# Router entry of a two-layer hybrid block: raw rows of x transposed, logits in four column groups from modulated weights, root and shift applied to the logits

## The reference, cut to what matters

```python
x_lat = x_lat + g1[:, None] * mix_x
hx2 = modulate(rmsnorm(x_lat, norm2_g[l]), sh2[:, None], sc2[:, None])   # h * (1 + scale) + shift
x_lat = x_lat + g2[:, None] * ec_moe(hx2, router_w[l], moe_w1[l], moe_w3[l], moe_w2[l])
...
aff = softmax(h @ router_w)                    # T x 16, fp32
gate, idx = top_k(swapaxes(aff, 1, 2), cap)    # cap = 32 tokens for each of 16 experts
```

## Time and profile before

| | |
|---|---|
| median of 3 runs | 2163.38 us (2161.03 to 2164.16) |
| profiled execution, span | 2163.4 us |
| TensorE busy | 1878.2 us, 87% |
| VectorE, ScalarE, GpSimd busy | 709.9, 444.8, 109.4 us |
| read from HBM | 560.27 MB, 259 GB/s over the span |

### The profile page before, as it was taken

One profiled execution on the slowest core, in us unless ns is written; L12 is line 12 of the kernel. 1 busy time (PEld: TensorE's weight loads), 2 busy tenths in 40 slices (PEclk: granted clock), 3 DMA queues, 4 the chain that ended last, 5 costly groups with the idle time before them and its releaser, 6 DMA issues.

```text
span 2163.4 us, 24879 instructions
## 1 busy us (share of the span) xinstructions
PE 1878.2 (87%) x9978; PEld 1123.9 (52%) x9978; DVE 709.9 (33%) x1130; ACT 444.8 (21%) x792; POOL 109.4 (5%) x150
## 2 busy tenths in 40 slices
PE   5999999999999799999999899999997666666654
PEld 3888756666777533333333488877886221112111
DVE  2273354433334512221222454455445100001001
ACT  2322333332222310000000332343333000000000
POOL 2070000000000000000000231000000000000000
PEclk9999999999999899999999999999999777778687
DMA  9423334234446489999999853444687899999996
GB/s 307 118 78 98 93 103 126 80 114 128 133 146 244 177 332 422 422 422 422 422 422 422 268 163 88 123 135 118 196 235 282 351 422 421 421 421 422 422 422 263
DMA packets 268871, 562.66 MB, mean 260 GB/s; under 512 B 11964, under 2 KB 208620, under 8 KB 219628
## 3 DMA queue, kind: packets, MB, share of 16 engines
q1 hardware_dynamic: 266412, 554.14, 68.2%
q0 software_dynamic: 1824, 5.12, 1.3%
q10 hardware_dynamic: 544, 2.10, 0.2%
HBM read 560.27 MB, written 1.05 MB: 259 GB/s over the span
## 4 chain that ended last, share of the span: by engine, by line
PE 68%; DMA 22%; DVE 5%; issue 2%; SPq 1%; ACT 1%; POOL 1%; POOLq 0%; DVEq 0%; ACTq 0%
PE PS L677 44%; PE PS L1096 17%; DMA nab<-in_moe_w 13%; DMA e_wr<-in_moe_w 6%; PE PS L738 2%; DMA ring<-in_w_mod 2%; PE PS L1047 2%; PE PS L871 1%; SPq L655 1%; DVE wr L1514 1%; PE PS L759 1%; PE PS L1074 0%; DVE arena L1560 0%; DVE arena L1819 0%; PE PS L1057 0%
## 5 line engine op out<-in xcount | busy, mean ns | idle before, releaser
L677 PE MATMUL PS<-hTr,wr 128*128 128x512 f32 (+1 forms) x2688 | 515.0, 348 | 5.2 <-DVE hTr L1548 5.2
L677 PEld LDWEIGHTS PS<-hTr,wr 128*128 128x128 f32 x2688 | 428.1, 190 | 72.5 <-issue 10.7
L1096 PE MATMUL PS<-arena 128*32 128x512 f32 (+1 forms) x960 | 305.1, 704 | 81.8 <-DMA nab<-in_moe_w 39.0
L1514 DVE TENSOR_TENSOR wr<-ring,wr 128x1024 fp32r<-128x1024 f32 x152 | 187.8, 1237 | 226.4 <-ACT wr L1162 226.2
L1162 ACT ACTIVATE wr<-ring 128x1024 fp32r<-128x1024 f32 x152 | 160.6, 1057 | 296.7 <-PE PS L677 279.4
L1096 PE MATMUL PS<-e_h,arena 128*64 128x512 f32 (+1 forms) x624 | 166.2, 702 | 49.1 <-DMA arena<-in_moe_w 43.3
L1096 PE MATMUL PS<-arena,e_h 128*64 128x512 f32 (+1 forms) x576 | 172.5, 711 | 33.1 <-DMA e_wr<-in_moe_w 17.0
L1096 PEld LDWEIGHTS PS<-arena 128*32 128x32 f32 (+1 forms) x960 | 82.9, 139 | 209.1 <-issue 204.3
L677 PE MATMUL PS<-wr,hTr 128*128 128x512 f32 x816 | 187.9, 390 | 4.1 <-DVE wr L1514 2.2
L677 PEld LDWEIGHTS PS<-wr,hTr 128*128 128x128 f32 x816 | 151.9, 188 | 37.7 <-DVE wr L1514 3.4
L1903 DVE TENSOR_TENSOR x<-x,PS 128x512 f32<-128x512 f32 x80 | 54.9, 687 | 238.7 <-PE PS L677 238.7
(11 more groups left out here) (170 smaller groups left out, 1923.4 us busy)
## 6 DMA issues: line engine op xcount, KB each, us to landing
arena<-in_moe_w SPq DMA_DIRECT2D x192, 1024.0 KB, 18.2
e_h<-in_moe_w SPq DMA_DIRECT2D x90, 1024.0 KB, 18.8
ring<-in_w_in SPq DMA_DIRECT2D x136, 512.0 KB, 4.8
e_wr<-in_moe_w SPq DMA_DIRECT2D x64, 1024.0 KB, 20.5
ring<-in_w_mod SPq DMA_DIRECT2D x96, 512.0 KB, 6.2
nab<-in_moe_w SPq DMA_DIRECT2D x32, 1024.0 KB, 21.8
ring<-in_w_br SPq DMA_DIRECT2D x64, 256.0 KB, 5.9
ring<-in_w_out SPq DMA_DIRECT2D x16, 512.0 KB, 4.4
```

The source lines that it names most:

```text
L677: return nc.tensor.matmul(o, a, b, start=first, stop=last)
L1096: ins = nc.tensor.matmul(PS[g * R:(g + 1) * R, bank + h, :], src[:, k, g * R:(g + 1) * R], space[:, kk * D + h * 512:kk * D + (h + 1) * 51 ...
L1514: nc.vector.tensor_tensor(wr[:, j % 2, 1, :], ring[:, slot, :], wr[:, j % 2, 0, :].bitcast(f32), ALU.subtract).then_inc(w_lo.sem, 1)
```

## The change

- x is transposed as it is, tile by tile, as soon as a tile's sum is there (`turn_rows`); ScalarE and VectorE copy the result to `xT`.
- The router's weights are multiplied by the scale once for each stream (`rwm`, VectorE). The logits of tile m are fp32 matmuls with 32 weight columns in column group m (`quarters`).
- The shift's part of the logits is computed apart, with one moving column, spread and transposed to `rconst`. VectorE multiplies the logits by 1/root and adds `rconst`.
- In layer 0 GpSimd does the first four residual adds.
- Normalised rows (`xn`) are made by ScalarE behind the exponentials; the gather waits for them.
- Slots 9 to 11 are freed with 7 and 8, since `hTr` isn't used any more.

The diff, cut to its core:

```diff
 # TensorE
-                for s in (7, 8):
+                for s in range(7, ESLOT):
                     pe.sem_inc(e_freed[s], 1)
-                pe.wait_ge(*mix_x.at(l, 2 * NT[l]))
-                transposes(2 * l + 1, tr_banks(2 * l + 1, NS))
-                pe.wait_ge(*rw_lo.at(l, 1))
-                for k in range(KD):
-                    if k % 2 == 0:
-                        pe.wait_ge(*h_lo.at(2 * l + 1, NS * (k // 2 + 1)))
-                    i = three(PS[:, 0, 0:tok], rwr[:, 0, k * E:k * E + 128], rwr[:, 1, k * E:k * E + 128],
-                              hTr[:, 0, k, 0:tok], hTr[:, 1, k, 0:tok], k == 0, k == KD - 1, False)
-                i.then_inc(logitsT.sem, 1)
...
+                def turn_rows(m):
+                    pe.wait_ge(*mix_x.at(l, 2 * m + 2))
+                    for k in range(KD):
+                        i = nc.tensor.transpose(PS[:, 2 * m + k // 4, k % 4 * 128:(k % 4 + 1) * 128],
+                                                paired(x[:, m, :], k), ident)
+                        if k % 4 == 3:
+                            i.then_inc(turned_x.sem, 1)
+                def quarters(bank, n, ms, weights, moving):
+                    for k in range(KD):
+                        for m in ms:
+                            i = nc.tensor.matmul(PS[32 * m:32 * m + 2 * E, bank, 0:n], weights(m, k), moving(m, k),
+                                                 start=(k == 0), stop=(k == KD - 1), tile_position=(0, 32 * m))
+                    return i
+                def row_logits(ms):
+                    return quarters(LB, 128, ms, lambda m, k: rwm[:, m // 2, k * E:(k + 2) * E],
+                                    lambda m, k: xT[:, m, k * 128:(k + 1) * 128])
+                pe.wait_ge(par_loaded, 16 * (l + 1))
+                pe.wait_ge(*rw_scaled.at(l, 1))
+                turn_rows(0)
+                turn_rows(1)
+                pe.wait_ge(*turned_act.at(l, 1))
+                quarters(0, 1, range(NT[l]), lambda m, k: par[:, P_RW + k * E:P_RW + (k + 2) * E],
+                         lambda m, k: modB[:, 1, m // 2, k:k + 1]).then_inc(shift_logits.sem, 1)
+                for m in range(2, NT[l]):
+                    turn_rows(m)
+                if NT[l] > 2:
+                    pe.wait_ge(*turned_act.at(l, 2))
+                    pe.wait_ge(*turned_dve.at(l, 2))
+                    row_logits((0, 1))
+                pe.wait_ge(*shift_spread.at(l, 1))
+                rows = 32 * NT[l]
+                nc.tensor.transpose(PS[:, 0, 0:rows], shT[0:rows, :], cst[0:rows, C_ID:C_ID + rows])\
+                    .then_inc(shift_turned.sem, 1)
+                pe.wait_ge(*turned_act.at(l, NT[l] - 1))
+                pe.wait_ge(*turned_dve.at(l, NT[l] + 1))
+                row_logits((NT[l] - 2, NT[l] - 1)).then_inc(logitsT.sem, 1)
+                pe.wait_ge(*logitsT_copied.at(l, 1))
+                nc.tensor.transpose(PS[:, LB, 0:rows], lgT[0:rows, :], cst[0:rows, C_ID:C_ID + rows])\
+                    .then_inc(logits.sem, 1)
...
+                pe.wait_ge(*xn_ready.at(2 * l + 1, NT[l]))
                 gather(0)
 # ScalarE
+                for m in range(NT[l]):
+                    square(2 * l + 1, m, (mix_x, l, 0))
+                    if m:
+                        turned_copy(m - 1)
+                    if m == max(1, NT[l] - 2):
+                        act.wait_ge(*shift_logits.at(l, 1))
+                        rows = 32 * NT[l]
+                        nc.scalar.activation(shT[0:rows, :], PS[0:rows, 0, 0:1].broadcast_to([rows, 128]), ACT.Copy)\
+                            .then_inc(shift_spread.sem, 1)
...
+                act.wait_ge(*logits.at(l, 1))
+                act.wait_ge(*rstd_done.at(2 * l + 1, NS))
+                for m in range(NT[l]):
+                    nc.scalar.activation(xn[:, m, :], x[:, m, :], ACT.Copy, scale=rstd[:, m:m + 1])\
+                        .then_inc(xn_ready.sem, 1)
 # GpSimd; pool_adds(l) is 2 * NT[l] - 4
+                for c in range(pool_adds(l)):
+                    m, h = c // 2, c % 2
+                    pool.wait_ge(*mix_gated.at(l, c + 1))
+                    xs_ = x[:, m, h * 512:(h + 1) * 512]
+                    pool.tensor_tensor(xs_, xs_, mix_tmp(c), ALU.add).then_inc(mix_x.sem, 1)
                 norm_roots(2 * l + 1, NS)
 # VectorE, in the loop over c
-                    if c:
+                    if c > pool_adds(l):
                         residual(c - 1)
                 residual(2 * NT[l] - 1)
-                for s in range(NS):
-                    normalise(2 * l + 1, s)
-                modulate(2 * l + 1, 1, NS)
+                for m in range(NT[l]):
+                    turned_copy(m, 1)
+                turned_copy(NT[l] - 1, 0)
+                dve.wait_ge(*logitsT.at(l, 1))
+                nc.vector.tensor_copy(lgT[0:rows, :], PS[0:rows, logits_bank(l), 0:128]).then_inc(logitsT_copied.sem, 1)
...
+                step(nc.vector.tensor_tensor(lg, rows_l, rstd[:, 0:NT[l]].unsqueeze(2).broadcast_to([128, NT[l], E]),
+                                             ALU.mult))
+                nc.vector.tensor_tensor(lg, lg, rconst[:, 0:NT[l], 0:E], ALU.add).then_inc(logits_ready.sem, 1)
```

More of the change, by code:

```diff
@@ L553, in build, with tr_banks, mod_pairs, logits_bank @@
         block = ctx.enter_context(nc.Block())
-        def tr_banks(nn, n_streams):
-            if nn == 0:
+        def tr_banks(l):
+            if l == 0:
                 return [(s, kp) for s in range(2) for kp in range(4)]
[L560 to L565, removed]
+            return [(s, kp) for kp in range(4) for s in range(2)]
+        def mod_pairs(l):
+            order = tr_banks(l)
+            return [(s, kp, order.index((s, kp))) for kp in range(4) for s in range(2)]
         def mod_bank(l, n):
             return 5 + n % 2 if l == 0 and n < MOD0 else 7
+        def logits_bank(l):
+            return 2 if NT[l] == 4 else 4
+        def pool_adds(l):
+            return 2 * NT[l] - 4
         def own(u, a, d):
@@ L770, in _ @@
                 if n == MOD0 - 2:
-                    transposes(0, tr_banks(0, 2)[0:4])
+                    transposes(0, tr_banks(0)[0:4])
             mod_post(0, MOD0 - 1)
@@ L777, in _ @@
                 tok = NS * T
-                transposes(2 * l, tr_banks(2 * l, 2)[4 if l == 0 else 0:])
+                transposes(l, tr_banks(l)[4 if l == 0 else 0:])
                 units, counts = WU[l]
@@ L1008, in _ @@
-                i.then_inc(logitsT.sem, 1)
-                pe.wait_ge(*logitsT.at(l, 1))
-                for s in (9, 10, 11):
-                    pe.sem_inc(e_freed[s], 1)
-                pe.wait_ge(*logits_copied.at(l, 1))
-                for m in range(NT[l]):
-                    i = nc.tensor.transpose(PS[:, 4, m * E:(m + 1) * E], work[0:E, 8, m * 128:(m + 1) * 128],
-                                            cst[0:E, C_ID:C_ID + E])
-                i.then_inc(logits.sem, 1)
+                def turn_rows(m):
[5 more added lines that the diff above has]
+                            i.then_inc(turned_x.sem, 1)
@@ L1162, in high, with square, modulate @@
                 nc.scalar.activation(wr[:, j % 2, 0, :], ring[:, slot, :], ACT.Copy).then_inc(w_hi.sem, 1)
+            def square(nn, m, written):
+                if written is not None:
+                    sig, layer, before = written
+                    act.wait_ge(*sig.at(layer, before + 2 * m + 2))
+                nc.scalar.activation(sil if nn % 2 == 0 else sq_junk, x[:, m, :], ACT.Square, accum_out=ss[:, m:m + 1])\
+                    .then_inc(sq_done.sem, 1)
+                act.wait_ge(*sq_done.at(nn, m + 1))
             def squares(nn, n_streams, written=None):
                 for m in range(2 * n_streams):
[L1166 to L1177 removed]
+                    square(nn, m, written)
+            def modulate(l):
+                act.wait_ge(*mod_ready.at(*MODULATED[l]))
+                pairs = mod_pairs(l)
                 def part_high(t):
                     if t % 2:
[L1181 removed]
+                        act.wait_ge(*tmp_dve.at(l, t // 2 + 1))
                     else:
[L1183 removed]
+                        act.wait_ge(*tmp_act.at(l, t // 2 + 1))
                     s, kp, _ = pairs[t]
```

119 lines of the change are left out of this document (67 added, 52 removed).

## The result

The changed kernel takes 2150.56 us (median of 4 runs, 2149.56 to 2152.32) against 2162.91 us (4 runs, 2161.03 to 2164.16). The medians are 12.35 us apart. The ratio of the runs is 0.9937, interval 0.9923 to 0.9951, which is 13.6 us less (10.6 to 16.7). 2153.7 was forecast, in a range of 2148.5 to 2159.0.

The account below looks back on a forecast made before the run. Expert weights stream at the DMA ceiling, so the router's chain ahead of them sets the time. Layer 0's 6.5 plus layer 1's 3.2 us make 9.7; 2163.4 less 9.7 is 2153.7 us, range 2148.5 to 2159.

Parts of the forecast that it names:

- The mechanism: Router ahead of the experts' weight stream: a microsecond cut from either layer's router is a microsecond of the run.
- Layer 0: Router of layer 0: last logits matmul at 734.5 us against 742.04, 7.5 us, less 1.0 for the clock: 6.5 us.
- The shift records: One-column matmuls for the shift's logits: 64 records in layer 0 at 0.05 us each, 3.2 us; 1.6 us in layer 1.
- my lower bound: Cheapest price for a shift record, from eight 32-column weight loads in 0.16 us: 0.02 us each, 1.3 us for 64.
- The start: Layer 0's first 16 transposes: from 723.1 to 724.9 us, right behind the output projection's end at 722.97, nothing waited for.
- The clock: TensorE's granted clock in layer 0's router: 3.4 us lost at half clock, nothing with no fall; 1.0 us taken.
- The row logits: Layer 0's logits matmuls of x, two tiles at a time: 1.7 us for each pair of tiles, plus drain.
- The tail: Layer 0, from the last logits matmul to the first exponential: 1.45 us against 1.39 before, counted as nothing.
- Layer 1: Router of layer 1, logits at half clock: 3.6 us less 0.4 for the tail, 3.2 us; 4.9 at full clock.
- The costs at nothing: Edits expected to cost nothing: GpSimd's adds, weight scaling, normalised rows, removed weight split, padding's memset, earlier loads on SyncE's queue.
- More: Rival, chance 0.16: no loss of clock in either layer, records at 0.02 to 0.03 us; 14.3 us gained, 2149.1.
- Slower: Rival, chance 0.04: one-column records don't overlap; 0.15 us each eats the gain, 0.31 us each gives 2178.7 us.

Follow-up runs that it names:

- late slots: The changed kernel, but weight slots 9 to 11 are freed only after the logits, as before the change; 2152.41 us, ratio 0.9924.
- the run with 512: The changed kernel with the one-column shift logits issued eight times over in both layers; 2182.66 us, ratio 1.0069.
- idle DMA engines: The kernel with the shift logits eight times over, but weight slots 7 to 11 freed only behind the logits; 2173.36 us in one run.
- the last version: The changed kernel with `e_freed` increments behind the first 16 transposes and layer 1's shift matmuls ahead of the output projection; 2151.53 us, ratio 0.9936.

## Why the prediction was right, step by step

**The mechanism** was right: the refill moves with the router, the run with the refill (0.98 us for each, over 13 traces), and the stream behind it is unchanged. The sizes were not: both layers gave more than forecast.

**Layer 0**, put at 6.5 us, gave 8.8. The logits' last matmul ends at +9.99 instead of +11.5. Three steps were mis-sized.
- *The shift records*, the dearest term: 0.05 us each, 3.2 us for 64. They took 0.71 us, 0.011 each, under even my lower bound of 0.02, which was a weight load with 32 columns elsewhere in the kernel. (My 3.2 + 0.14 from 724.9 ends at 728.24, not 728.4; the slip is 0.16 us.) In layer 1, with two groups, a record took 0.67 / 32 = 0.021 us. With the change of form, for which nothing shows in the trace, 3.5 us became 0.64 (726.89 to 727.53): 2.9 us to the good. The Trainium skill (TensorEngine Tiling (Array Packing), Instruction Overhead) would make it an estimated 1.6 us; it was nearer than I was, and still more than twice too dear, so the measurement decides. For its other rule, that a change of tiling mode drains the array (Key Properties), no price can be read here: the shift's records begin at 726.89, 0.07 us before the modelled end of the transposes (724.80 + 2.16), and so does the next change, at 727.53 against 727.60.
- *The start*: +1.08 instead of +0.13. I had counted no time for the increments on TensorE's queue. 0.95 us to the bad. The 32 transposes add 0.6 (4.2 us against 3.6). With 0.2 that I had for a wait on VectorE's copies, and which is not there: 11.5 + 0.95 + 0.6 - 2.9 - 0.2 = 10.0.
- *The clock*: I took 1.0 us off for a partial fall. In the trace it is 1.00 from 725 to 735 us. The row logits were right: 1.94 us a set, and 4.07 from the first to the last end, against 4.1. The tail is 1.64 us, not 1.45.

**Layer 1**, put at 3.2 us, gave 6.1 in the profiled execution. I had assumed the half clock and named 4.9 for the full one; the profile fell on full clock (row logits 1.94 us), and there the shift was 0.67 us instead of 1.6. In the profiles of the runs with late slots and with all adds on VectorE, whose layer 1 is the same up to the logits (but for three semaphore increments), these took 3.41 and 3.30 us; their refills stand at +34.73 and +34.97, a gain of 4.3 to 4.5 us over before. So the case I forecast does occur, and gives 4.3 to 4.5 us where I had 3.2. Again the shift was too dear: 0.67 and 1.02 us in these two, not 1.6. With such a layer 1 both layers give about 13.2 us, which is nearer to the runs' 12.35 (medians) and 13.6 (ratio) than the 14.9 of the changed kernel's own profile.

**The costs at nothing** held: GpSimd's adds, the early loads, the normalised rows, the products for the router's weights (two in 0.49 us under the projection).

**The sum.** The two terms gave 9.7; 14.9 are in the profiles, 12.35 between the medians of the runs. The gain was put a fifth to a third too low, and most of that is the price of the shift's records (2.9 us in layer 0, 0.9 in layer 1). I made the sum against the span of 2163.4 and took it for the run's time. With the 1.8 us around it, that execution was 2165.2, and the same sum would have said 2155.5, further off. The two errors are of opposite sign, and that 2153.7 comes within 3.1 us of the runs is in part luck.

**The rivals.** "More" (2149.1: no loss of clock, records at 0.02 to 0.03) describes the profile better than my forecast does in its two reasons, and the runs' 2150.56 are nearer to it than to my 2153.7, though just inside the forecast's own range of 2150.5 to 2157. I had given "more" 0.16. "Slower" needed 0.15 us a record; they took 0.011. But the run with 512 shows another way to be slower that I had not thought of: many small instructions in a row end in a pause of 5 us. The change, with 64 such records in a row, shows no pause there.

## What to carry to other kernels

When a chain of small steps stands ahead of a saturated stream, cost it in microseconds of the chain and ask which value it waits for: here a root was moved from the entry of the chain to its end, and with the same work but a wait for that root nothing clear of the runs' noise is gained. Count the clock with the wait: in layer 0 TensorE paid for a stand of 5.8 us with 3.8 more in the matmuls behind it. And put matmuls of different column groups next to each other in the queue: a one-column record then cost 0.011 us here, and 0.030 group by group.

## What was unexpected of the hardware

- **Pauses of TensorE in long runs of small instructions**: in layer 0 every 256 instructions (128 records and their loads), 4.9 to 5.1 us with the DMA engines at 1.02, 1.8 to 2.3 us with them at 0.00; in layer 1, at 0.025 to 0.029 us a record against 0.009 to 0.017, one of 1.91 us and none. That they are waits for the instructions themselves fits this and the 6 further packets of the instruction queue, but is argued, not shown.
- **A 32-column record with one moving column costs 0.008 to 0.011 us** at full clock with four column groups side by side, 0.021 with two, and 1.89 / 64 = 0.030 if each group's records stand together.
- **A semaphore increment by itself on TensorE's queue costs about 0.15 us**: the first transpose of layer 0 at +1.08, +0.64, +0.31 and +0.06 with six, three, one and none ahead of it (`chunk_sum`'s counted; changed kernel, late slots, idle DMA engines, the last version).
- **The half clock falls in one execution and not in another, at the same work.** Layer 1's row logits took 1.94 us in the profiles of the changed kernel and of two experiments, and 3.26 to 3.63 in eight others. Three of these (all adds on VectorE, rows before the exponentials, TensorE busy through the top-k) have the same TensorE instructions in that layer up to there. In the one with all adds on VectorE TensorE stood 1.50 us, ran the first eight transposes at 1.00 and fell to the half clock in the stand of 0.71 us behind them; in the changed kernel it stayed at 1.00 through stands of 1.51 and 0.71. What decides it stays open; dummy work helped in the wait for the root and didn't in the gather.
